# Gate and up of a gated feed-forward by seven block products instead of eight

## What is computed

```
h2 = _rms_norm(x, norm_ffn)
gate_pre = h2 @ w_gate
gate_c, new_ffn = _causal_dwconv(gate_pre, ffn_hist, ffn_conv_w)
x = x + (jax.nn.silu(gate_c) * (h2 @ w_up)) @ w_down
```

## Time and profile before

| | |
|---|---|
| median of 3 executions | 1770.08 us (1770.01 to 1772.39) |
| the profiled execution: its time / its span | 1770.14 us / 1768.3 us |
| mean granted TensorE clock | 0.992 |
| busy: TensorE matmul, weight load | 1692.9 us (96%), 1469.5 us (83%) |
| busy: VectorE, ScalarE, GpSimd | 877.9 us (50%), 532.8 us (30%), 137.1 us (8%) |
| HBM traffic | 90 GB/s over the span |

### The profile page before, as it was taken

One profiled execution on the slowest core, in us unless ns is written; L12 is line 12 of the kernel. 1 busy time (PEld: TensorE's weight loads), 2 busy tenths in 40 slices (PEclk: granted clock), 3 DMA queues, 4 the chain that ended last, 5 costly groups with the idle time before them and its releaser, 6 DMA issues.

```text
span 1768.3 us, 27996 instructions
## 1 busy us (share of the span) xinstructions
PE 1692.9 (96%) x10758; PEld 1469.5 (83%) x10758; DVE 877.9 (50%) x1400; ACT 532.8 (30%) x921; POOL 137.1 (8%) x360
## 2 busy tenths in 40 slices
PE   7989998899999999999998999989999999999998
PEld 6757796678999999999886677866899999999997
DVE  4335437535555555545544454565265545445554
ACT  3213427414222222222332133364242222222221
POOL 1103200101000000000011021000010000000000
PEclk9999999999999999999999999999999999999999
DMA  8204330831222222222241224318222222222222
GB/s 246 60 10 110 115 118 25 276 108 53 79 82 74 81 71 71 82 72 71 81 108 58 54 71 131 120 47 277 72 72 72 81 73 71 74 80 71 71 73 75
DMA packets 125025, 160.77 MB, mean 91 GB/s; under 512 B 25604, under 2 KB 77262, under 8 KB 124622
## 3 DMA queue, kind: packets, MB, share of 16 engines
q1 hardware_dynamic: 124808, 159.44, 29.3%
q10 hardware_dynamic: 144, 0.33, 0.1%
HBM read 150.22 MB, written 9.53 MB: 90 GB/s over the span
## 4 chain that ended last, share of the span: by engine, by line
PE 92%; ACT 3%; DVE 2%; issue 1%; DVEq 1%; DMA 1%; POOL 0%; SPq 0%; POOLq 0%; ACTq 0%
PE bank L1653 87%; PE bank L1715 5%; ACT pf L1073 1%; DMA raw<-in_w_in 1%; DVEq L1516 1%; DVE n L1381 0%; POOL small L804 0%; DVE wlo L1169 0%; ACT pTf L978 0%; DVE xn L1198 0%; ACT lrows L1158 0%; DVE small L1506 0%; ACT xn L962 0%; ACT ps L1106 0%; ACT rT L978 0%
## 5 line engine op out<-in xcount | busy, mean ns | idle before, releaser
L1653 PE MATMUL bank<-hhi,whi 128*128 128x320 f32 (+1 forms) x1632 | 505.5, 310 | 0.0
L1653 PE MATMUL bank<-hlo,whi 128*128 128x320 f32 (+1 forms) x1632 | 505.0, 309 | 0.0
L1653 PE MATMUL bank<-hhi,wlo 128*128 128x320 f32 (+1 forms) x1632 | 504.9, 309 | 0.0
L1169 DVE TENSOR_TENSOR wlo<-raw,whi 128x1024 fp32r<-128x1024 f32 (+1 forms) x204 | 245.7, 1207 | 349.0 <-ACT whi L926 348.0
L926 ACT ACTIVATE whi<-raw 128x1024 fp32r<-128x1024 f32 (+1 forms) x204 | 211.8, 1042 | 419.7 <-PE bank L1653 407.5
L1653 PEld LDWEIGHTS bank<-hhi,whi 128*128 128x128 f32 (+1 forms) x1632 | 303.9, 186 | 2.6
L1653 PEld LDWEIGHTS bank<-hlo,whi 128*128 128x128 f32 (+1 forms) x1632 | 303.8, 186 | 2.7
L1653 PEld LDWEIGHTS bank<-hhi,wlo 128*128 128x128 f32 (+1 forms) x1632 | 303.8, 186 | 1.8
L1653 PE MATMUL bank<-whi,hhi 128*128 128x512 f32 x560 | 226.5, 404 | 7.5 <-DVE n L1367 2.7
L1653 PE MATMUL bank<-wlo,hhi 128*128 128x512 f32 x560 | 220.5, 394 | 0.0
L1653 PE MATMUL bank<-whi,hlo 128*128 128x512 f32 x560 | 220.4, 394 | 0.0
(11 more groups left out here) (203 smaller groups left out, 1503.8 us busy)
## 6 DMA issues: line engine op xcount, KB each, us to landing
raw<-in_w_in SPq DMA_DIRECT2D x52, 512.0 KB, 3.8
raw<-in_w_gate SPq DMA_DIRECT2D x44, 512.0 KB, 3.8
raw<-in_w_up SPq DMA_DIRECT2D x44, 512.0 KB, 3.8
raw<-in_w_down SPq DMA_DIRECT2D x44, 512.0 KB, 3.5
vb<-in_cache_fox_v SPq DMA_DIRECT2D x16, 1024.0 KB, 7.6
raw<-in_w_out SPq DMA_DIRECT2D x16, 512.0 KB, 4.7
kb<-in_cache_fox_k SPq DMA_DIRECT2D x8, 1024.0 KB, 7.0
kbo<-in_cache_fox_k SPq DMA_DIRECT2D x8, 1024.0 KB, 6.9
```

The source lines that it names most:

```text
L1169: dve.tensor_tensor(wlo[:, s_, 0:w_], raw[:, s_, 0:w_], whi[:, s_, 0:w_].bitcast(F32), ALU.subtract).then_inc(lo_split, 1)
L1653: return pe.matmul(out, lhsT=lhsT, rhs=rhs, start=start, stop=stop, skip_group_check=True)
```

## The change

In the ten looped pairs, the 1024 x 256 block of gate (and of up) is cut in four: Axy is the 128-column tile x with the k half y (512 rows). The tokens are cut in four too: Byz is the k half y with the token half z (320 tokens). Seven products of such blocks (`WINO`) take the place of eight. Each has 4 k tiles and 3 matmuls with 320 columns: 12 matmuls.

- **Token sums**, once per layer before the loop: T1 = B12 - B11, T2 = B22 - T1, T3 = B22 - B12, T4 = B21 - T2. VectorE first adds high and low parts back to four whole blocks h11, h12, h21, h22 (`whole`), makes T1 and T2, and GpSimd makes T3 and T4. ScalarE makes the four high parts (`t_high`), VectorE the four low parts (`t_low`). TensorE and ScalarE's first part of a weight block wait for the last of them.
- **Weight sums**, eight per turn on GpSimd (`weight_sums`): S1 = A21 + A22, S2 = S1 - A11, S3 = A11 - A21, S4 = A12 - S2, 128 x 512 each. They wait for both loaded slabs.
- **Splits** are of blocks of 128 x 512: seven for gate, seven for up, and down's two slabs of 128 x 1024. They stand in a ring of nine blocks (whi and wlo, 6, and new xhi and xlo, 3). The raw ring keeps its three slots, and loads wait for named low parts ("events": 0 to 6 gate, 7 and 8 down, 9 to 15 up).
- **Banks.** Products a1, a2, a3 and a4 pile up in one bank that is read in between: a1 must be copied before a2 may start, a2 before a3, and VectorE must have added a3 before a4 starts. c1 and c2 pile up in another bank. ScalarE copies the first contribution of each output, VectorE adds the second in SBUF (`added`).
- **Product and convolution.** up is gathered in gu and multiplied by the silu in SBUF, its last quarter straight from the bank. The first convolution tap moves from VectorE to ScalarE (`first_tap`). GpSimd's sums for up stand ahead of its wait for the convolution, those for the next gate behind it.
- The loop is nine turns and one written out behind it.

```diff
+WINO = (("a1", "A11", "B11"), ("c1", "S1", "T1"), ("a2", "S2", "T2"), ("b1", "A12", "B21"), ("a3", "S3", "T3"),
+        ("c2", "S4", "B22"), ("a4", "A22", "T4"))
+WINO_BANKS = {"g": {"a": 0, "b": 1, "c": 2}, "u": {"a": 3, "b": 2, "c": 1}}
+WINO_OUT = {"a1": (0, 0), "b1": (0, 0), "c1": (1, 1), "a3": (1, 1), "a2": (0, 1), "c2": (0, 1), "a4": (1, 0)}
+WINO_SUMS = (("S1", 1), ("S2", 2), ("S3", 4), ("S4", 5))
+RING = (6, 7, 8, 2, 3, 4, 5, 0, 1)
...
-    banks.loop(PAIRS - 1, [(("g", "loop", i // 2, i % 2), i) for i in range(4)] + down_jobs()
-   + [(("u", "loop", i // 2, i % 2), U_BANKS[i]) for i in range(4)])
+    banks.loop(PAIRS - 1, wino_jobs("g") + down_jobs() + wino_jobs("u"))
...
+    def ffn_loads(it, further):
+        for j, e in ((3, 4), (4, 6), (5, 7)):
+            load(LOOP0 + j, l, ffn_src(j, it), (e, it))
+        for j, e in ((0, 8), (1, 13), (2, 15)) if further else ():
+            load(LOOP0 + j, l, ffn_src(j, it + 1), (e, it))
...
+    def weight_sums(kind, it, before):
+        other = "u" if kind == "g" else "g"
+        for j in range(2):
+            wait_loaded(pool, LOOP0 + (0 if kind == "g" else 4) + j, l, it)
+            apart(pool)
+        for name, out, x_, y_, op in (("S1", s1, quarter(kind, "A21"), quarter(kind, "A22"), ALU.add),
+                                      ("S2", s2, by_k(s1[:, :]), quarter(kind, "A11"), ALU.subtract),
+                                      ("S3", s3, quarter(kind, "A11"), quarter(kind, "A21"), ALU.subtract),
+                                      ("S4", s4, quarter(kind, "A12"), by_k(s2[:, :]), ALU.subtract)):
+            if before is not None:
+                wait_lo(pool, wino_event(other, dict(WINO_SUMS)[name]), l, before)
+                apart(pool)
+            pool.tensor_tensor(by_k(out[:, :]), x_, y_, op).then_inc(s_sum, 1)
+            if name in ("S1", "S3"):
+                pool.drain()
...
+    pool.tensor_tensor(h12[:, :, :], h22[:, :, :], h12[:, :, :], ALU.subtract).then_inc(t_sum, 1)
...
+    pool.tensor_tensor(h21[:, :, :], h21[:, :, :], t2f[:, :, :], ALU.subtract).then_inc(t_sum, 1)
+    weight_sums("g", 0, None)
...
+    def ffn_side(it, further):
         ffn_pads(it * 2 + 4)
-        pool.wait_ge(gconv, l * (2 * PAIRS) + it * 2 + 4)
+        weight_sums("u", it, it)
+        pool.wait_ge(gconv, it * 2 + (l * (2 * PAIRS) + 4))
         apart(pool)
         ffn_last(it * 2 + 4)
+        if further:
+            weight_sums("g", it + 1, it)
...
+    upto(G0 + 3, l)
+    def t_high(i, name):
+        act.wait_ge(*((t3_sum, l * 2 + i // 2 + 1) if i in (0, 2) else (t_sum, l * 2 + i // 2 + 1)))
+        act.activation(t_hi_lo[name][0][:, :, :], t_full[name][:, :, :], ACT.Copy).then_inc(t_hi, 1)
     gate("pro")
-    upto(G0 + 4, l)
+    for i, name in enumerate(("T1", "T3", "T2", "T4")):
+        t_high(i, name)
     silu(l * (2 * PAIRS))
...
+    act.wait_ge(t_lo, l * 4 + 4)
+    for i in range(7):
+        if i == 3:
+            B.wait_full(act, ("g", "pro", 1, 1), l)
+        if i == 5:
+            wait_used(act, G0 + 2, l)
+        part_hi("g", i, l, 0)
+    B.wait_full(act, ("u", "pro", 1, 1), l)
+    down_hi(0, l, 0)
...
+        copied("g", "a1", it)
+        act.wait_ge(gu_done, it + (l * PAIRS + 1))
         act.activation(guhi[:, :, :], gu[:, :, :], ACT.Copy).then_inc(gu_hi, 1)
...
+        copied("g", "c1", it)
+        B.wait_full(act, ("g", "loop", "c1"), l, it)
+        down_hi(1, l, it)
+        copied("g", "a2", it)
+        for i in range(4):
+            up_hi(i, l, it)
+        copied("g", "a4", it)
+        B.wait_taken(act, ("g", "loop", "c2"), l, it)
+        act.wait_ge(gpad_hist, it + (l * PAIRS + 2))
+        first_tap(0, it)
+        act.drain()
+        first_tap(1, it)
+        up_hi(4, l, it)
+        silu(it * 2 + (l * (2 * PAIRS) + 2), [0])
+        up_hi(5, l, it)
+        silu(it * 2 + (l * (2 * PAIRS) + 2), [1])
+        up_hi(6, l, it)
...
+            gate_hi(0, l, it)
+            copied("u", "a1", it)
+            gate_hi(1, l, it)
+            gate_hi(2, l, it)
+            copied("u", "c1", it)
+            gate_hi(3, l, it)
+            copied("u", "a2", it)
+            for i in range(4, 7):
+                gate_hi(i, l, it)
+            B.wait_full(act, ("u", "loop", "a4"), l, it)
+            down_hi(0, l, it + 1)
...
+    dve.drain()
+    whole(h12, "B12")
+    whole(h11, "B11")
+    whole(h22, "B22").then_inc(h_full, 1)
+    dve.drain()
+    dve.tensor_tensor(h11[:, :, :], h12[:, :, :], h11[:, :, :], ALU.subtract).then_inc(t3_sum, 1)
+    whole(h21, "B21").then_inc(h_full, 1)
+    dve.drain()
+    dve.tensor_tensor(t2f[:, :, :], h22[:, :, :], h11[:, :, :], ALU.subtract).then_inc(t3_sum, 1)
+    gate_conv("pro", 0)
+    t_low(0, "T1")
+    gate_conv("pro", 1)
+    for i, name in ((1, "T3"), (2, "T2"), (3, "T4")):
+        t_low(i, name)
+    for i in range(5):
+        part_lo("g", i, l, 0)
...
+        dve.wait_ge(gu_hi, it + (l * PAIRS + 1))
+        lo(gulo[:, :, :], gu[:, :, :], guhi[:, :, :]).then_inc(gu_ready, 1)
+        down_lo(1, l, it)
+        part_lo("u", 0, l, it)
+        B.wait_taken(dve, ("g", "loop", "a1"), l, it)
+        added("g", "b1", it)
+        part_lo("u", 1, l, it)
+        B.wait_taken(dve, ("g", "loop", "c1"), l, it)
+        added("g", "a3", it)
+        part_lo("u", 2, l, it)
+        B.wait_taken(dve, ("g", "loop", "a2"), l, it)
+        added("g", "c2", it)
+        part_lo("u", 3, l, it)
+        other_taps(0, it)
+        part_lo("u", 4, l, it)
...
+        down_add(0)
+        down_add(1)
         dve.drain()
...
+        other_taps(1, it)
+        for n in range(2, 5):
+            down_add(n)
+        part_lo("u", 5, l, it)
+        part_lo("u", 6, l, it)
+        for n in range(5, 2 * TT):
+            down_add(n)
         dve.drain()
...
+        def gate_lo(i):
+            if further:
+                part_lo("g", i, l, it + 1)
+        for i in range(3):
+            gate_lo(i)
+        B.wait_taken(dve, ("u", "loop", "a1"), l, it)
+        added("u", "b1", it)
+        gate_lo(3)
+        B.wait_taken(dve, ("u", "loop", "c1"), l, it)
+        added("u", "a3", it)
+        gate_lo(4)
+        B.wait_taken(dve, ("u", "loop", "a2"), l, it)
+        added("u", "c2", it)
+        gate_lo(5)
+        dve.drain()
+        dve.wait_ge(gsilu, it * 2 + (l * (2 * PAIRS) + 4))
+        for out_of, in_of, ft, t0, t1 in ((plain(gu), conv_out(gact), 0, 0, SEQ),
+                                          (plain(gu), conv_out(gact), 1, HALF, SEQ),
+                                          (plain(gu), conv_out(gact), 0, None, None),
+                                          (plain(gu), conv_out(gact), 1, None, None)):
+            dve.tensor_tensor(out_of(ft, t0, t1), out_of(ft, t0, t1), in_of(ft, t0, t1), ALU.mult)
+        gate_lo(6)
+        key = ("u", "loop", "a4")
+        B.wait_full(dve, key, l, it)
+        dve.tensor_tensor(gu[:, 1, 0:HALF], bank[B.bank(key)][:, 0:HALF], gact[:, 1, 0:HALF],
+                          ALU.mult).then_inc(B.free[B.bank(key)], 1)
+        dve.drain().then_inc(gu_done, 1)
+        if further:
+            down_lo(0, l, it + 1)
...
+    def products(kind, it):
+        for i, (name, _, tokens) in enumerate(WINO):
+            key = (kind, "loop", name)
+            wait_lo(pe, wino_event(kind, i), l, it)
+            B.wait_room(pe, key, l, it)
+            out = bank[B.bank(key)][:, 0:HALF]
+            s_ = wino_block(kind, i)
+            hi, lo_ = t_hi_lo[tokens]
+            for k in range(4):
+                ws = slice(P * k, P * k + P)
+                ins = mm3(out, part(True, s_)[:, ws], part(False, s_)[:, ws], hi[:, k, :], lo_[:, k, :],
+                          k == 0 and name[1] == "1", k == 3)
+            fill(ins, key)
...
+    pe.wait_ge(t_lo, l * 4 + 4)
     with pe.Fori(0, PAIRS - 1) as it:
...
+        products("g", it)
+        down(it)
+        products("u", it)
```

More of the change, by code:

```diff
@@ L69 @@
 DLAST = SLABS - 2
+EV = 16
+EV_LAST = LOOP0 + EV * (PAIRS - 1)
+EVENTS = EV_LAST + 2
 assert SLABS % SLOTS == 0 and 6 % SLOTS == 0
@@ L1607, in gate_conv @@
                     conv(gact, gpad, ft, lambda j: ftap[:, ft, j:j + 1]).then_inc(gconv, 1)
-                def product(wait, done):
-                    dve.drain()
-                    dve.wait_ge(gsilu, done)
-                    for i in range(4):
-                        wait(i)
-                        mul_bank(plain(gu), ("u", "pro", i // 2, i % 2), conv_out(gact)).then_inc(B.free[U_BANKS[i]], 1)
-                gate_conv("pro", 0)
-                upto(G0 + 4, l)
-                gate_conv("pro", 1)
@@ new lines, in _ @@
+                t_low(0, "T1")
[5 more added lines that the diff above has]
+                dve.drain()
+                dve.wait_ge(gsilu, l * (2 * PAIRS) + 2)
+                for i in range(4):
+                    key = ("u", "pro", i // 2, i % 2)
+                    B.wait_full(dve, key, l)
```

(27 more changed lines are left out.)

287 lines of the change are left out of this document (196 added, 91 removed).

## The result

The changed kernel is slower: 1798.12 us median (1794.37 to 1799.32, 4 executions) against 1771.24 us for the kernel before in the same session (1770.01 to 1773.76, 4 executions). The ratio is 1.015, with a 95% interval of 1.0138 to 1.0162. The forecast was 1746 us, and its range ended at 1780.

A forecast was written before the change was run, and what follows sets the result against it. TensorE's own stream was taken to bound the kernel: 1770.1 - 70.4 (removed matmuls) + 20 (waits in turns) + 24 (entering the loop, first turn included) + 2.4 (leaving it) = 1746 us, range 1724 to 1780.

The forecast's parts named there:

- Removed matmuls: In the loop, 24 fewer matmuls of 320 columns per turn, 3.52 us; over twenty turns -70.4 us.
- The path of the wait: Each turn, a4 waits for a3's addition behind down's low part, load, S1 and up's low part: 1.0 us, 20 in all.
- VectorE's low part 0.7 ...: 10.5, and 0.26 for GpSimd beside it: On the chain to a4, S1's low part ends at 10.5 us, or 10.8 with 0.26 us lost to GpSimd.
- I charge four collisions of 0.26: Before the loop, VectorE beside GpSimd's T3 and T4: its row of work moves from 1330.2 to 1331.2.
- rival 1: VectorE and GpSimd exclude each other fully: 36 us of waits in the turns, 47 at the entries; 1785 us, chance 0.17.
- the load of up's second slab, 3.8: On the chain to a4, this load takes 3.8 us and ends at 7.45 us after gate's start.
- The charge of the clock: TensorE begins the loop at 1.2 GHz after standing; its first product takes 3.2 us for 1.76, charged nothing.
- Before the loop: TensorE stands 8 us in each layer, waiting for the low part of T4 and the first gate part.
- the first turn, which I had 4 us over the others: First turn's a4 ends 16.9 us after the first product, later turns' 13.3; 4 us more with the copies' waits.
- After the loop: Two slab splits on VectorE ahead of gulo and a later product cost 1.2 us per layer, 2.4 us in all.

The follow-up runs named there:

- experiment 6: Changed kernel with the additions of a3 and c2 first, low parts and taps spread between down's additions: 1740.77 us, ratio 0.9832 to the kernel before.
- Experiment 5: Changed kernel with GpSimd multiplying one raw quarter by 1.0 in place of each weight sum (does not compute the layer): 1774.07 us, one execution.
- experiment 2: Changed kernel with the split of G0+3 behind T2 on VectorE and gate's four weight sums ahead of T3 and T4 on GpSimd: 1783.3 us, ratio 1.0064.

## Why the prediction was wrong

- **Removed matmuls: right.** The distance stayed 0.147 us, and the turn of experiment 6 is 38.61 us for the calculated 38.65. The 70.4 us are there.
- **The path of the wait: right in place and order.** With t = 0 at 1485.85, down's low part ended at 3.6 (predicted 3.6). Then it drifts: S1 began at 8.6 (7.75, because the load took 4.4 us, not the 3.8 of the earlier trace rows), the low part of S1 ended at 12.0 (10.8), and a4 began at 12.6 (11.5). It is 2.0 us late, not 1.0.
- **The step that failed: "VectorE's low part 0.7 ...: 10.5, and 0.26 for GpSimd beside it"**, and with it "I charge four collisions of 0.26" before the loop. Measured: 0.76 for that low part, and 2.6 us at t2f and 2.7 at the first tap. I had one row for each direction and took the price of the second, from an operation with one tensor input, for sums with two, though I wrote down that they differ. In the turn this is 0.5 us of the 1.9 by which the turn overran my forecast; before the loop it is the larger part. Experiment 5 shows what it is worth: where GpSimd lets go early, the low part of S1 takes 0.79 us, and the kernel 24 us less, which is still 28 over the forecast. The rival that I gave 0.17 named this mechanism, but took the other terms from my forecast. The rule of the Trainium skill (SBUF — State Buffer, "SBUF: two separate sides"), an exclusive lock kept for the whole instruction, holds here for two-input sums (S2: all but 0.14 us) and for GpSimd's turn to wait (1.28 us for a copy of 0.19), but not for the multiplication by a scalar (0.46 of 1.49 us).
- **A term that was too small: "the load of up's second slab, 3.8".** On the chain it took 4.6 us on average (19 turns, 4.1 to 5.0), so it is 0.8 us of the overrun in each turn, more than the collision. In the turn shown it is issued 1.8 us behind up's first load, where the kernel before had 7.1 us between the two. That the closeness is the cause is read from the trace; no run changes it.
- **The charge of the clock: wrong in place.** I looked for its cost only at the loop's first block, where I charged nothing. It fell behind four of the 20 waits before a4, which cost 6 us in all; why behind these and not behind others as long stays open. Turns are 2.9 us over 38.65: 2.0 of recorded wait, 0.5 beside it and 0.35 from the clock. That makes 58 us in place of 20, and even rival 1 (36) was short.
- **Before the loop:** TensorE is held up 15.3 us in place of 8, twice, because T2 and the taps wait for T3, T4 and the four weight sums (9 us for the 1.0 that I charged); 15 us more in all. About 9 of the 15.3 were avoidable by order alone (experiment 2).
- **After the loop: right in kind, a little too much.** Down began 5.0 us after the start of the last up matmul, for 4.25 before: 0.8 per layer in place of 1.2. The two slab splits and gulo stand in line, 2.36 and 1.41 us.
- **Sum:** the loops 36 us more than forecast (38 from the turns; the first turn, which I had 4 us over the others, came to about 3), the stands 15 more, the exits 1 less: 50 us, against 1799.3 - 1746 = 53. The other 3 us lie outside these places, 1.3 of them ahead of the first loop and 1.8 between the layers, and are not explained.

What stays open: why a multiplication by a scalar lets go early; what makes the loads on the chain longer; what decides whether the clock falls behind a wait of some 2.2 us; T3 and T4 on VectorE in the changed kernel's own order wasn't tried; nor was anything against the last 4.5 us of stand per layer.

## What to carry to other kernels

Work given to an idle GpSimd is not free for VectorE: look for the operations with two SBUF inputs that it will meet, price each meeting at the rest of GpSimd's operation, and take the price only from a row of the same kind of operation. Where an in-order engine has an addition that TensorE waits for, put it ahead of everything whose input is still on its way; here this, with the low parts and taps spread behind it so that down's additions came in time, turned +1.5% into -1.7%. Moving the additions alone gave 15 of the 57 us. Take the time of a load on such a chain from loads that follow each other as closely as they will there. And a new wait can cost more than its length: here 0.5 us in every turn, and a stretch at the lower clock behind four waits of twenty.

## What the runs showed of the hardware

- A GpSimd sum of 128 x 512 (two inputs) takes 1.27 to 1.29 us undisturbed, a multiplication by a scalar of the same size 1.49, a copy 0.61. The sum kept VectorE out until 0.14 us before its recorded end, the multiplication for 0.46 us; for the copy it was not worked out.
- VectorE's addition to x from a PSUM bank, with only one input in SBUF, kept its 0.68 us beside the same sums (the longest of 220 took 0.69, and five in a row took 3.12 us at 1512.31, while GpSimd made S3 and S4):

```profile
L1807 DVE TENSOR_TENSOR x<-x,bank 128x512 f32<-128x512 f32 x220 | 139.2, 679 | 23.7 <-PE bank L1977 23.4
```

- But a VectorE operation with one tensor input and both its sides in SBUF (the first tap) did lose time, 3.25 us for 0.56, beside GpSimd's two-input T4.
- Pauses of TensorE of 3.35, 2.36, 2.24 and 2.19 us before a4 were followed by some 3 us or more at 1.2 GHz; six others of 2.19 to 2.46 us, and all shorter ones, were not.
